# Sixty-four sample tokens of an expert's down product: from four column tiles of 32 tokens to two of 64

## The reference, cut to what matters

```python
def _expert_choice(h, w_router, w_gate, w_up, w_down):
    n_tok, d = h.shape
    cap = CAPACITY_FACTOR * n_tok // N_EXPERTS          # 32 (prompt), 64 (sample)
    aff = jax.nn.softmax((h @ w_router).astype(jnp.float32), axis=-1)
    gate, idx = lax.top_k(aff.T, cap)
    xe = h[idx]
    hid = jax.nn.silu(jnp.einsum("ecd,edf->ecf", xe, w_gate)) * jnp.einsum("ecd,edf->ecf", xe, w_up)
    ye = jnp.einsum("ecf,efd->ecd", hid, w_down) * gate[..., None].astype(h.dtype)
    return jnp.zeros_like(h).at[idx.reshape(-1)].add(ye.reshape(-1, d))
```

## Time and profile before

| what | value |
|---|---|
| median of 3 runs | 1172.59 us (1171.43 to 1172.86) |
| profiled execution, its own time | 1173.55 us |
| span from first to last instruction of it | 1171.6 us |
| mean granted TensorE clock, share of full | 0.965 |
| PE busy | 1057.4 us (90%) |
| PE loads of stationary operands busy | 600.2 us (51%) |
| DVE, ACT, POOL busy | 441.1, 255.4, 287.7 us |
| DMA moved | 254.00 MB |
| `gate_up`, L1933, busy (two groups) | 170.7 and 171.1 us |
| `down`, L1945, busy (two groups) | 87.9 and 85.9 us |
| scatter, L683 on POOL | 48 DMAs, 75.0 us |

### The profile page before, as it was taken

The page is one execution under the profiler, slowest core; times in us unless marked ns, Lnnn a source line. Parts: engine busy times, 40 slices in busy tenths (PEclk is TensorE's granted clock), DMA queues, the critical chain, the costliest instruction groups (busy, mean ns, idle before and its releaser), DMA issues.

```text
span 1171.6 us, 20620 instructions
## 1 busy us (share of the span) xinstructions
PE 1057.4 (90%) x8753; PEld 600.2 (51%) x8753; DVE 441.1 (38%) x872; ACT 255.4 (22%) x534; POOL 287.7 (25%) x311
## 2 busy tenths in 40 slices
PE   5999778878999899898999999999999999999940
PEld 3568667665565587665633334444443334444420
DVE  5436785447777876675100101111101101111018
ACT  1143334266556611320110000000000000000002
POOL 0006994234554200000100212221012212220134
PEclk9999998979999999999999999999999999999975
DMA  9010200200000531404189999999999999999854
GB/s 339 14 51 22 72 1 1 74 34 1 1 1 1 170 127 54 180 27 180 41 333 400 391 386 391 384 398 401 388 390 399 390 385 387 394 399 404 325 157 176
DMA packets 63116, 254.00 MB, mean 217 GB/s; under 512 B 7383, under 2 KB 15447, under 8 KB 46686
## 3 DMA queue, kind: packets, MB, share of 16 engines
q1 hardware_dynamic: 52542, 234.48, 51.3%
q0 software_dynamic: 10528, 18.88, 6.5%
HBM read 237.62 MB, written 15.73 MB: 216 GB/s over the span
## 4 chain that ended last, share of the span: by engine, by line
PE 67%; DVE 13%; DMA 9%; POOL 6%; issue 2%; ACT 2%; SPq 0%; DVEq 0%; POOLq 0%; ACTq 0%
PE ps L1933 24%; PE ps L1945 11%; DMA ring<-in_w_e_up 7%; PE ps L1574 4%; PE ps L1680 2%; PE ps L1695 2%; PE ps L1568 2%; PE ps L1828 1%; PE ps L1785 1%; PE ps L1787 1%; PE ps L1786 1%; PE ps L1813 1%; PE ps L1814 1%; PE ps L1815 1%; DVE xT L1467 1%
## 5 line engine op out<-in xcount | busy, mean ns | idle before, releaser
L1933 PE MATMUL ps<-ring,mix 128*32 128x512 f32 x1536 | 170.7, 592 | 2.1 <-DMA ring<-in_w_e_up 2.1
L1933 PE MATMUL ps<-late,mix 128*32 128x512 f32 x1536 | 171.1, 593 | 0.0
L1419 DVE TENSOR_TENSOR mix<-mix,ps 128x768 f32<-128x768 f32 x16 | 15.3, 954 | 323.0 <-ACT mix L996 323.0
L996 ACT ACTIVATE mix<-ps 128x768 f32<-128x768 f32 x16 | 13.0, 811 | 480.3 <-PE ps L1933 480.3
L1933 PEld LDWEIGHTS ps<-ring,mix 128*32 128x32 f32 x1536 | 49.6, 110 | 117.9 <-issue 111.9
L1933 PEld LDWEIGHTS ps<-late,mix 128*32 128x32 f32 x1536 | 48.1, 110 | 109.1 <-issue 106.8
L1945 PE MATMUL ps<-late,mix 128*32 128x256 f32 x1536 | 87.9, 385 | 2.8 <-DMA late<-in_w_e_down 2.8
L1945 PE MATMUL ps<-ring,mix 128*32 128x256 f32 x1536 | 85.9, 379 | 0.0
L1426 DVE TENSOR_SCALAR mix<-ps,att 128x256 f32<-128x256 f32 x48 | 20.3, 478 | 161.7 <-PE ps L1945 161.7
L683 POOL DMA_INDIRECT acc_rows<-mix,idx_now x48 | 75.0, 1562 | 20.5 <-POOL idx_now L691 10.7
L1945 PEld LDWEIGHTS ps<-late,mix 128*32 128x32 f32 x1536 | 49.9, 111 | 35.5 <-DVE mix L1413 3.2
(11 more groups left out here) (295 smaller groups left out, 1793.0 us busy)
## 6 DMA issues: line engine op xcount, KB each, us to landing
late<-in_w_e_gate SPq DMA_DIRECT2D x32, 1024.0 KB, 19.2
late<-in_w_e_up SPq DMA_DIRECT2D x32, 1024.0 KB, 21.3
ring<-in_w_e_gate SPq DMA_DIRECT2D x32, 1024.0 KB, 18.7
ring<-in_w_e_up SPq DMA_DIRECT2D x32, 1024.0 KB, 20.9
late<-in_w_e_down SPq DMA_DIRECT2D x16, 2048.0 KB, 22.3
ring<-in_w_e_down SPq DMA_DIRECT2D x16, 2048.0 KB, 22.2
ring<-in_w_in SPq DMA_DIRECT2D x3, 2048.0 KB, 9.0
late<-in_w_ple_gate SPq DMA_DIRECT2D x2, 2048.0 KB, 14.1
```

What stands on the lines that cost most here:

```text
L1933: last = nc.tensor.matmul(ps[32 * j:32 * (j + 1), GU + g, :].rearrange("p (w c) -> p w c", w=2), xeT[:, k, 32 * g:32 * (g + 1)], gu_w[q][: ...
```

## The change

The prompt group stays as it is: 32 tokens, four column tiles, 256 streamed columns, quarter rows. The two sample groups become one of 64 tokens: two column tiles of 64 columns each, 512 streamed columns, half rows. In `down` each slice k now issues the four narrow matmuls and then the two wide ones (`down_step(0, ..)`, `down_step(1, ..)`). The sample result lies in one PSUM bank of 512 columns. `ye_out` has two instructions (256 and 512 wide), `scatter` two indirect DMAs: 128 rows of 1 KB and 128 rows of 2 KB. Row numbers and gates are laid out to match; the memsets of `jcol` double, and the products that spread them over the partitions go from 24 to 12.

```diff
@@ row numbers and views
-        hid, ye = [r.rearrange("p (i c) -> p i c", i=NG3) for r in rows[2:4]]
-        acc_quarters = acc_rows.rearrange("t (j c) -> (t j) c", j=CT)
+        hid = rows[2].rearrange("p (i c) -> p i c", i=NG3)
+        ye = (rows[3][:, 0:256], rows[3][:, 256:768])
+        acc_parts = (acc_rows.rearrange("t (j c) -> (t j) c", j=4), acc_rows.rearrange("t (j c) -> (t j) c", j=2))
...
             def scatter():
-                for i in range(NG3):
-                    pool.indirect_dma_start(acc_quarters,
+                for i in range(NSC):
+                    pool.indirect_dma_start(acc_parts[i],
                                             bass.IndirectOffsetOnAxis(ap=idx_now[:, 1 + i:2 + i], axis=0),
-                                            ye[:, i, :], None, compute_op=ALU.add).then_inc(s_scat, 16)
+                                            ye[i], None, compute_op=ALU.add).then_inc(s_scat, 16)
...
-                for i in range(NG3):
-                    last = nc.vector.tensor_scalar(ye[:, i, :], ps[:, DN + i, 0:256], gate4[:, i, at_e], None,
-                                                   ALU.mult)
+                for i, w in enumerate((256, 512)):
+                    last = nc.vector.tensor_scalar(ye[i], ps[:, DN + i, 0:w], gate4[:, i, at_e], None, ALU.mult)
...
+            def down_step(g, k, src, w):
+                rows = (32, 64)[g]
+                cols = D * rows // P
+                for j in range(P // rows):
+                    last = nc.tensor.matmul(ps[rows * j:rows * (j + 1), DN + g, 0:cols], src[:, k, ROWS[g]],
+                                            w[:, cols * j:cols * (j + 1)], start=(k == 0), stop=(k == KD - 1))
+                return last
+
             def down_half(e, d, src):
                 pe.wait_ge(s_dnw[d], 16 * (e + 1))
                 for i in range(4):
-                    k = 4 * d + i
-                    for g in range(NG3):
-                        for j in range(CT):
-                            last = nc.tensor.matmul(ps[32 * j:32 * (j + 1), DN + g, 0:256],
-                                                    src[:, k, 32 * g:32 * (g + 1)],
-                                                    dn_w[d][:, i, 256 * j:256 * (j + 1)],
-                                                    start=(k == 0), stop=(k == KD - 1))
+                    down_step(0, 4 * d + i, src, dn_w[d][:, i, :])
+                    last = down_step(1, 4 * d + i, src, dn_w[d][:, i, :])
                 last.then_inc(s_ud, 1)
```

More of the change, by code:

```diff
@@ L75, in hymba_layer @@
     NG3 = CAP // 32
+    NSC = 2
+    ROWS = (slice(0, CAPP), slice(CAPP, CAP))
+    assert (CAPP, CAPS) == (32, 64)
     PADW = TP * P + TS * P + 6
@@ L126, in hymba_layer @@
         topi = sb("topi", [NE, CAP], U32)
-        jcol = sb("jcol", [P, 1])
-        idx4 = sb("idx4", [P, NG3, NE], I32)
+        jcol = sb("jcol", [P, NSC])
+        idx4 = sb("idx4", [P, NSC, NE], I32)
         idxT = sb("idxT", [CAP, NE], I32)
-        idx_now = sb("idx_now", [P, 1 + NG3], I32)
+        idx_now = sb("idx_now", [P, 1 + NSC], I32)
         qksq = sb("qksq", [P, 640])
@@ L193, in hymba_layer @@
         Z_PARTS = [(2, 6), (6, 8), (0, 2)]
-        gate4 = att[:, 0, 0:NG3 * NE].rearrange("p (i e) -> p i e", i=NG3)
+        gate4 = att[:, 0, 0:NSC * NE].rearrange("p (i e) -> p i e", i=NSC)
         rows = [mixf[:, D + i * KD * CAP:D + (i + 1) * KD * CAP] for i in range(4)]
         xeT, hidT = [r.rearrange("p (k c) -> p k c", k=KD) for r in rows[0:2]]
-        hid, ye = [r.rearrange("p (i c) -> p i c", i=NG3) for r in rows[2:4]]
-        acc_quarters = acc_rows.rearrange("t (j c) -> (t j) c", j=CT)
+        hid = rows[2].rearrange("p (i c) -> p i c", i=NG3)
+        ye = (rows[3][:, 0:256], rows[3][:, 256:768])
+        acc_parts = (acc_rows.rearrange("t (j c) -> (t j) c", j=4), acc_rows.rearrange("t (j c) -> (t j) c", j=2))
         QC = D // (2 * P)
@@ L546, in _ @@
                 load_dn(NE - 1, d)
-            sp.wait_ge(s_scat, 16 * NG3 * NE)
+            sp.wait_ge(s_scat, 16 * NSC * NE)
             for t in range(NT):
@@ L569, in _ @@
             for j in range(CT):
-                ch.link(nc.gpsimd.memset(jcol[32 * j:32 * (j + 1), :], float(j)))
+                ch.link(nc.gpsimd.memset(jcol[32 * j:32 * (j + 1), 0:1], float(j)))
+                ch.link(nc.gpsimd.memset(jcol[32 * j:32 * (j + 1), 1:2], float(j // 2)))
             for c0, w in ((0, 2), (2 + TP * P, 2), (4 + T, 2)):
@@ L690, in pick_quarters @@
             def pick_quarters(e):
-                return nc.gpsimd.tensor_copy(idx_now[:, 1:1 + NG3].unsqueeze(2), idx4[:, :, bass.ds(e, 1)])
+                return nc.gpsimd.tensor_copy(idx_now[:, 1:1 + NSC].unsqueeze(2), idx4[:, :, bass.ds(e, 1)])
             pool.wait_ge(s_xeT_p, 2)
@@ L711, in _ @@
                 scatter()
-            pool.wait_ge(s_scat, 16 * NG3 * NE)
+            pool.wait_ge(s_scat, 16 * NSC * NE)
             for t in range(NT - 1):
@@ L1402, in _ @@
             nc.vector.tensor_copy(idxT[:], ps[0:CAP, 5, 0:NE]).then_inc(s_idx, 1)
-            nc.vector.tensor_scalar(idx4[:].rearrange("p i e -> p (i e)"), ps[:, 5, NE:(1 + NG3) * NE], float(CT), jcol[:, 0:1],
-                                    ALU.mult, ALU.add).then_inc(s_idx, 1)
-            nc.vector.tensor_copy(att[:, 0, 0:NG3 * NE], ps[:, 5, (1 + NG3) * NE:(1 + 2 * NG3) * NE]).then_inc(s_idx, 1)
+            for i, parts in enumerate((4, 2)):
+                last = nc.vector.tensor_scalar(idx4[:, i, :], ps[:, 5, (1 + i) * NE:(2 + i) * NE], float(parts),
+                                               jcol[:, i:i + 1], ALU.mult, ALU.add)
+            last.then_inc(s_idx, 1)
+            nc.vector.tensor_copy(att[:, 0, 0:NSC * NE], ps[:, 5, (1 + NSC) * NE:(1 + 2 * NSC) * NE]).then_inc(s_idx, 1)
             for u in range(7, 2 * NT):
@@ L1423, in ye_out @@
                 if not first:
-                    dve.wait_ge(s_scat, 16 * NG3 * e)
-                for i in range(NG3):
-                    last = nc.vector.tensor_scalar(ye[:, i, :], ps[:, DN + i, 0:256], gate4[:, i, at_e], None,
-                                                   ALU.mult)
+                    dve.wait_ge(s_scat, 16 * NSC * e)
+                for i, w in enumerate((256, 512)):
+                    last = nc.vector.tensor_scalar(ye[i], ps[:, DN + i, 0:w], gate4[:, i, at_e], None, ALU.mult)
                 last.then_inc(s_ye, 1)
@@ L1897, in _ @@
             for v, src in enumerate((topf, topv)):
-                for i in range(NG3):
-                    c = (1 + v * NG3 + i) * NE
-                    for j in range(CT):
-                        last = nc.tensor.matmul(ps[32 * j:32 * (j + 1), 5, c:c + NE], src[:, i * 32:(i + 1) * 32],
+                for i in range(NSC):
+                    c = (1 + v * NSC + i) * NE
+                    w = ROWS[i].stop - ROWS[i].start
+                    for j in range(P // w):
+                        last = nc.tensor.matmul(ps[w * j:w * (j + 1), 5, c:c + NE], src[:, ROWS[i]],
                                                 ident[0:NE, 0:NE], start=True, stop=True)
```

## The result

| | before | after |
|---|---|---|
| median of the runs, us | 1172.58 (1171.43 to 1172.86, 4 runs) | 1203.16 (1202.42 to 1205.27, 4 runs) |
| ratio | 1 | 1.0266 (95% interval 1.0248 to 1.0283) |
| profiled execution, us (span) | 1173.55 (1171.6) | 1205.27 (1203.5) |

A forecast was written before the change was run, and what follows sets the result against it. PE was taken to set the pace, the weight stream just behind. Width changes 34.5, less 2.75 of waits, 2.1 at the end and 1.4 in the tail, gave +28.2 us: 1200.8 us predicted, likeliest case 1196 to 1209.

The forecast's parts named there:

- What bounds the kernel: Expert phase: PE sets the pace at 33.10 us per expert, so time added in `down` is paid in full, less waits.
- Streaming: Sample part of a `down` slice: 0.86 us before and after, counted at nothing if wide tiles stream side by side.
- third rival: In `down`, the two wide tiles do not stream side by side: 110 us more, about 1311 us; chance 0.06.
- The width changes: In `down`: 0.16 us into a 64-wide piece, 0.125 back, 2.16 per `down`, 34.5 us together.
- the first load of 64 columns: First matmul behind a change into wide tiles in `down`: 0.05 us longer, between 0.025 and 0.105.
- first rival: In `down`, only changes into 64-wide tiles cost, 20.5 us; net +14.6, 1187 us; chance 0.10.
- the second (none): In `down`, no change between column-tile widths costs; 1168.4 to 1171.2 us, say 1169.8; chance 0.12.
- What the waits give back: Expert phase: PE's period rises to 35.26 us, the weight stream no longer falls behind, and 2.75 us of waits return.
- a pace of 34.08 us: Weight stream in the expert phase: the period at which it can go, read from two periods with refills in the chain.
- The end of the phase: Last expert: 3.4 us counted, 2.9 returned if the clock stays full, 1.25 if it falls; 2.1 taken.
- PE resumes at 8.8: Last expert: PE goes on 8.8 us after the first half load's issue; the new wait is 1.6 us.
- The tail: Behind the last matmul: one scatter issue and 0.14 us of DVE less, last transfer 0.6 more; 1.4 us less.

The follow-up runs named there:

- e2_group: The changed kernel with each half's four slices grouped by width, 2 width changes per `down` instead of 15; 1174.78 us, ratio 1.0010 to the kernel before.
- e1_narrow_half: The changed kernel with its half rows kept but the sample products in four 32-wide tiles, no width changes; 1171.99 us, ratio 0.9985 to the kernel before.
- e5_index_narrow: `e1_narrow_half` with the products that spread row numbers and gates in 32-wide tiles too; 1169.86 us, ratio 0.9974 to the kernel before.

## Why the prediction was right, point by point

**What bounds the kernel.** Right: the 2.13 us added to PE's `down` came out in the period in full.

**Streaming.** Right: 0.43 and 0.86 us of each 1.58 us slice, as forecast; `e2_group` and `e1_narrow_half` show it without the changes. The third rival is out.

**The width changes.** Right in mechanism and size, term by term. Forecast were stops of 0.11 us on leaving narrow tiles and 0.10 on leaving wide ones; measured are 0.105 and 0.10. With the first load behind it, a change into the wide tiles costs 0.16 and one back 0.125, as forecast, and one `down` 2.13 us more instead of 2.16. The term that I had bounded most loosely, the first load of 64 columns, is 51 ns, between the 25 and the 105 of the earlier trace rows: the longest matmul, a wide one behind a change, takes 643 ns where a plain matmul over 512 columns takes 592. Matmuls by line (ns min/median/max, first and last start, forms):

```profile
L1950 PE MATMUL ps<-ring,mix x768: 379/403/643, 645.9 to 1161.2; 128*32 128x256 f32 x128, 128*64 128x512 f32 x64
```

The narrow matmuls show the same in small: 403 ns behind a change, 379 otherwise. The first rival (one direction alone) and the second (none) are out by the timeline of PE above, and the count of changes (2, 7, 15) by 0.145 us each on average gives `down` in three kernels. The rule of the Trainium skill, page TensorEngine Tiling (Array Packing), section Key Properties, says that a change of the tiling mode drains TensorE. The trace agrees for 32 and 64 columns as far as it shows the stop, 0.10 us; what the array does during it no row shows.

**What the waits give back.** Right: the two slow periods of the earlier trace rows are gone. Together with the width changes ahead of the end the forecast was 34.5 - 3.4 - 2.75 = 28.3 us; the table has 28.4. That close an agreement is in part luck: the changed kernel has a wait of 0.4 us for the first experts' weights that I had not counted, and the changes came out a little cheaper. The reason that I gave, a pace of 34.08 us at which the stream can go, is not borne out: `e2_group` ran 13 periods of 33.35 us without a wait for refills.

**The end of the phase.** Right that most of the lengthening hides there, wrong in what PE waits for. The step that failed is "PE resumes at 8.8": it resumed 1147.52 - 1138.07 = 9.45 us after the issue. The loads went as forecast; the second was issued at 1145.19 - 1138.07 = 7.1 and the slower of the two took 8.3. But VectorE scales the sums of `down(14)` (1.14 us) and then copies the hidden values (1.01 us), and PE may go on only behind the copy. This takes 2.4 us from the end of `down(14)`, in the changed kernel as in `e1_narrow_half` and `e5_index_narrow`, where `down` is no longer than before. I had looked at the load alone, which in the kernel before was the later of the two by 0.2 us, and so let the wait shrink to 1.6 us, below what VectorE allows. Of the two outcomes that I gave for the clock, the worse came:

```profile
1148.20:1151.40 3.20, 3.20 (x14) 0.68 (x16) 0.00 (x0) 0.00 (x0) 1.97 (x2) 0.50 1.01 388
```

I had taken the middle of both. The end came out 2.6 us longer where 1.3 were forecast (3.4 counted less 2.1 returned): half of the error is the later start, the other half the clock. Only 0.8 of the 3.4 were given back, below my bound of 1.25.

**The tail.** Right in sign, 0.8 us less instead of 1.4. What was mis-sized is the last transfer. The landing of the scatters in the tail (L688, from 1160 to 1172 us):

```profile
DMA to landing us min/median/max: 3.8/4.4/5.0
```

The 1 KB rows land 3.8 us after their issue, the 2 KB rows 5.0: 1.2 us more, the upper end of my 0 to 1.2, where I had taken 0.6. In the profiles of the six experiments the last scatter, also of 2 KB rows, lands after 4.6 to 4.9 us, so 0.8 to 1.2 more is what these runs show.

**What was missing.** The stretch ahead of the experts, +2.4 us, was not in the sum at all: 0.5 us were there at PE's first matmul already (12.74 against 12.24 us), 0.2 are the products that spread the row numbers (0.95 us until PE goes on behind them, against 0.73), and about 1.7 are the fallen clock. Against the profiled executions the sum is short by 31.9 - 28.2 = 3.7 us, of which this is 2.4, the end 1.3 and the tail 0.6, less the 0.7 of the last stage. Against the medians it is short by 30.6 - 28.2 = 2.4; the executions behind the medians have no profile each, so this difference is not split up.

## What to carry to other kernels

Do not alternate the column-tile width inside a loop on PE: run all steps of one width, then all of the other, or pair token halves with column halves so that the wide layout comes out of narrow tiles. Here the cost was the number of changes times 0.145 us, with 2, 7 and 15 changes. Before counting what a wait will hide, list everything that the waiting engine needs at that point and when each would arrive. In the kernel before, VectorE's copy came 0.2 us ahead of the load and did not show; in the changed kernel it decided, and taking it away bought 0.3 us, because the load was next. A clock that differs between two profiles is not shown to be an effect of the change until it differs again in a second kernel with the same code.

## What the hardware showed that I had not expected

The stop at a width change is nearly the same in both directions (0.105 us on leaving the narrow tiles, 0.10 on leaving the wide ones); what differs is the first matmul behind it, 51 ns longer for 64 columns and 24 ns for 32. Scatters of 2 KB rows land 0.8 to 1.2 us later than those of 1 KB rows with the same number of rows (4.6 to 5.0 against 3.8 us). The granted clock fell to 0.50 for about 3.4 us behind the same 2.03 us pause of PE in one kernel and not in another with the same instructions of PE around it; a pause of 2.03 us alone therefore does not tell what the clock will do.
